# The first loads in another order, and the second mixer's output projection in split matmuls with part of its weight preparation on GpSimd

## The reference

```python
def first_block(x, ...):
    h = rmsnorm(x, mix_pre_g)
    u, v_s, q, k, v_a, g_a, g_b, f_logit = jnp.split(h @ w_in, IN_SPLITS, axis=-1)
    y_a = spatial_gating(gelu(u), gelu(v_s), w_spatial, b_spatial, sgu_norm_g)
    y_b = forgetting_attention(q, k, v_a, f_logit, b_forget)
    x = x + rmsnorm((sigmoid(g_a) * y_a + sigmoid(g_b) * y_b) @ w_out, mix_post_g)
    return x + rmsnorm(swiglu(rmsnorm(x, ffn_pre_g), w_gate, w_up, w_down), ffn_post_g)

def second_block(x, mem, ...):
    hn = rmsnorm(x, norm_mix_g)
    u_pool, m_q, m_k, m_v, m_o, m_i, m_f, a_q, a_k, a_v = jnp.split(hn @ w_in_2, ...)
    y_pool  = pool_mixer(u_pool, pool_w, pool_scale)           # width 256
    y_mlstm = mlstm_mixer(m_q, m_k, m_v, m_o, m_i, m_f, ...)   # width 256
    y_attn  = attn_mixer(a_q, a_k, a_v, ...)                   # 8 query heads of 64, 2 key heads, rotated
    x = x + jnp.concatenate([y_pool, y_mlstm, y_attn], axis=-1) @ w_out_2   # the projection that changes
    x = x + mem_cross_attn(rmsnorm(x), mem, ca_wq, ca_wkv, ca_wo)
    x = x + ec_moe(rmsnorm(x), router_w, w_gu, w_down)         # 16 experts, 32 tokens each
    return rmsnorm(x, final_norm_g)
```

## Time and profile before

| | |
|---|---|
| runs | 1501.70, 1501.83, 1503.94 us (median 1501.83) |
| profiled execution | 1501.2 us, its span 1499.4 us, mean granted clock 0.875 |
| busy share of the span | PE 81%, its weight load 48%, DVE 27%, ACT 20%, GpSimd (POOL) 3% |
| DMA | 500.9 MB, 334 GB/s over the span |
| chain that ended last | PE 49%, DMA 46%, DVE 2%, ACT 1% |

### The profile page before, as it was taken

How to read it: one execution, slowest core, us unless ns; L and a number is a source line. 1 busy time by engine, 2 the same in 40 slices (tenths; PEclk the granted TensorE clock), 3 DMA queues, 4 the chain that set the end, 5 groups by cost and what they waited for, 6 DMA issues and landing times.

```text
span 1499.4 us, 16367 instructions
## 1 busy us (share of the span) xinstructions
PE 1220.6 (81%) x7015; PEld 713.6 (48%) x7015; DVE 404.0 (27%) x601; ACT 307.0 (20%) x433; POOL 37.8 (3%) x41
## 2 busy tenths in 40 slices
PE   8999999999999999986775775776757857757675
PEld 7888888888878566332231331331322313313232
DVE  5756465665367654000000000000000000000001
ACT  5544444444265552000000000000000000000001
POOL 1000000000031100000000000000000000000000
PEclk9999999999999999886787778778878687787799
DMA  9745436555544388999999999999999999999996
GB/s 340 264 169 170 167 113 206 188 176 218 195 142 128 110 324 345 420 428 429 426 427 427 427 428 428 427 429 427 427 427 429 427 429 427 427 427 428 427 427 283
DMA packets 85347, 500.91 MB, mean 334 GB/s; under 512 B 4990, under 2 KB 30020, under 8 KB 60596
## 3 DMA queue, kind: packets, MB, share of 16 engines
q1 hardware_dynamic: 84084, 495.60, 81.9%
q0 software_dynamic: 1216, 4.63, 0.9%
HBM read 499.16 MB, written 1.05 MB: 334 GB/s over the span
## 4 chain that ended last, share of the span: by engine, by line
PE 49%; DMA 46%; DVE 2%; ACT 1%; issue 0%; POOL 0%; SPq 0%; POOLq 0%; DVEq 0%; ACTq 0%
DMA arena<-in_expert_w_gu_dram 34%; DMA arena<-in_expert_w_down_dram 11%; PE psA L655 9%; PE psB L1346 5%; PE psB L1299 4%; PE psB L888 4%; PE psA L694 4%; PE psB L694 3%; PE psB L1256 3%; PE psA L698 2%; PE psA L1071 2%; PE psB L698 2%; PE psA L899 1%; PE psA L666 1%; PE psA L1006 1%; PE psA L1135 1%
## 5 line engine op out<-in xcount | busy, mean ns | idle before, releaser
L1299 PE MATMUL psB<-arena,x_res 128*32 128x512 f32 x2048 | 323.9, 766 | 200.8 <-DMA arena<-in_expert_w_gu_dram 200.8
L1299 PEld LDWEIGHTS psB<-arena,x_res 128*32 128x32 f32 x2048 | 63.1, 125 | 432.7 <-DMA arena<-in_expert_w_gu_dram 311.1
L1853 DVE TENSOR_TENSOR split_r<-arena,split_r 128x2048 fp32r<-128x2048 f32 x75 | 171.7, 2292 | 109.9 <-ACT split_r L1387 109.6
L1737 ACT ACTIVATE x_res<-psB 128x512 f32<-128x512 f32 x16 | 9.6, 597 | 840.6 <-PE psB L1299 840.6
L1387 ACT CAST split_r<-arena 128x2048 fp32r<-128x2048 f32 x76 | 145.0, 1912 | 102.5 <-PE psA L655 52.7
L655 PE MATMUL psA<-split_r,hT_r 128*128 128x512 f32 x664 | 154.2, 391 | 0.0
L1346 PE MATMUL psB<-arena 128*32 128x512 f32 x1008 | 143.0, 723 | 10.2 <-DMA arena<-in_expert_w_down_dram 9.9
L655 PEld LDWEIGHTS psA<-split_r,hT_r 128*128 128x128 f32 x664 | 123.7, 188 | 25.5 <-issue 0.2
L1256 PE MATMUL psB<-sb_b,arena 128*128 (+1 forms) x512 | 104.7, 382 | 11.4 <-ACT arena L1739 11.3
L1256 PEld LDWEIGHTS psB<-sb_b,arena 128*128 128x128 f32 x512 | 102.4, 310 | 17.8 <-issue 14.2
L2381 DVE TENSOR_TENSOR x_res<-x_res,psB 128x512 f32<-128x512 f32 x16 | 16.4, 1026 | 282.7 <-ACT x_res L1737 282.7
(11 more groups left out here) (396 smaller groups left out, 1086.9 us busy)
## 6 DMA issues: line engine op xcount, KB each, us to landing
arena<-in_expert_w_gu_dram SPq DMA_DIRECT2D x128, 2048.0 KB, 35.3
arena<-in_expert_w_down_dram SPq DMA_DIRECT2D x62, 2048.0 KB, 36.2
arena<-in_w_in_dram SPq DMA_DIRECT2D x35, 1024.0 KB, 7.8
arena<-in_w_gate_dram SPq DMA_DIRECT2D x11, 1024.0 KB, 5.5
arena<-in_w_up_dram SPq DMA_DIRECT2D x11, 1024.0 KB, 8.1
arena<-in_w_down_dram SPq DMA_DIRECT2D x10, 1024.0 KB, 6.6
arena<-in_w_out_dram SPq DMA_DIRECT2D x6, 1024.0 KB, 6.2
arena<-in_ca_wkv_dram SPq DMA_DIRECT2D x4, 1024.0 KB, 6.2
```

The costliest lines, as they stand in the source:

```text
L1299: ins = pe.matmul(psB[32 * j:32 * j + 32, o, :], XC[:, k, :], w[4 * o + j], start=(k == 0), stop=(k == GU_SLOTS - 1), skip_group_check=True)
L1853: v.tensor_tensor(W_LO[n % 2].rearrange("p (k n) -> p k n", **shape), view, W_HI[n % 2].bitcast(F32).rearrange("p (k n) -> p k n", **shape ...
```

## The change

It does these things:

- **Start.** `WS` is loaded after `u0` instead of ahead of the constants. GpSimd issues the forget bias, the forget weights and the second block's gate weights first, then the first gain; it waits for these and for `WS` and the constants, and issues the second gain, the broadcast rows, the router and the pool weights after that. DVE's wait before the gate split is for three small transfers (the wait for all six is further on). ACT begins with a Square of one element. PE's first pass takes the high and the low operand of each half before the next half.
- **Projection.** `wout20` and `wout21` (column halves) become `w2a` and `w2b` (row blocks, 1024 wide, four rows each in two pieces). Each row is 12 split matmuls of 512 columns: high and low weights with the high operand `YT`, high weights with the low operand `YL`. DVE makes `YL` (`rest`). The order of the rows is 0, 1, 4, 5, 6, 7, 2, 3.
- **Who splits them.** `w2a/0`: high ACT, low GpSimd. `w2a/1` and `w2b/0`: high and low GpSimd. `w2b/1`: high ACT, low DVE. `wq` is split in two steps, the second after the operand of the cross attention.
- **Order on PE.** The queries are transposed ahead of the band product, the keys behind it. The pool's product goes to another bank. The keys move to another tile (`KK`).
- **Expert loads.** The last dense load (`wo`) is issued after expert load 0; load 3 waits for `w2b`'s low parts, load 4 for `wq`'s.

The core of the diff:

```diff
@@ loads (SP)
+        w = A["w_out_2"][0]
+        for name, k0, i0, at0 in (("w2a", 0, 0, 0), ("w2b", 2, 2, 2)):
+            add(name, ..., halves=D)
+        W2_ROW = {0: ("w2a", 0, 0), 1: ("w2a", 0, 1), 4: ("w2a", 1, 0), 5: ("w2a", 1, 1),
+                  6: ("w2b", 0, 0), 7: ("w2b", 0, 1), 2: ("w2b", 1, 0), 3: ("w2b", 1, 1)}
...
             load(0)
             load(1)
-            sp.dma_start(WS, A["w_spatial_t"]).then_inc(sig("consts_loaded"), 16)
             sp.dma_start(cst[:, P:NCONST], A["consts"][:, P:NCONST]).then_inc(sig("consts_loaded"), 16)
             for i in range(2, N_DENSE - 1):
                 load(i)
                 if i == 2:
+                    sp.dma_start(WS, A["w_spatial_t"]).then_inc(sig("consts_loaded"), 16)
...
             sp.wait_ge(sig("pool_mm"), 2)
             expert_load(0)
+            load(N_DENSE - 1)
             sp.wait_ge(sig("ym_ready"), 1)
             expert_load(2)
             sp.wait_ge(sig("ym_tr"), 1)
             expert_load(1)
+            for n, _ in pieces["w2b"]:
+                sp.wait_ge(*lo_signal(n))
+            expert_load(3)
             sp.wait_ge(*lo_signal(pieces["wq"][-1][0]))
-            expert_load(3)
-            load(N_DENSE - 1)
-            after_slot(sp, "wout21")
             expert_load(4)
@@ PE
-                for k in range(h):
-                    pe.wait_ge(sig("xh_ready"), k // 2 + 1)
-                    pe.wait_ge(*((sig("first_cast"), 1) if k < h // 2 else (sig("hi_ready"), 1)))
-                    for t in range(TT):
-                        pe.matmul(psA[:, 2 * pair + t, :], HTS[0][:, k, t * P:(t + 1) * P], w[:, k, :], ...)
+                for b, quarter in enumerate(("first_cast", "hi_ready")):
+                    pe.wait_ge(sig(quarter), 1)
+                    for i, x_ready in enumerate(("xh_ready", "xl_ready")):
+                        pe.wait_ge(sig(x_ready), b + 1)
+                        for k in (2 * b, 2 * b + 1):
+                            for t in range(TT):
+                                pe.matmul(psA[:, 2 * pair + t, :], HTS[i][:, k, t * P:(t + 1) * P], w[:, k, :], ...)
...
+            pe.wait_ge(sig("aq_ready"), 2)
+            pe.wait_ge(sig("rope_ready"), 2)
+            pe.wait_ge(sig("om_ready"), ML_H)
+            for i in range(4):
+                for t in range(TT):
+                    ins = pe.transpose(psB[:, i // 2, ...], RQ[:, t, i, :], ident)
...
             def at_turn(i):
-                if i >= 1:
-                    pe.wait_ge(sig("yt_ready"), 1 + i)
+                pe.wait_ge(sig("xl_ready"), YL_FIRST + 1 + i)
...
             def merged_rows(k, count):
+                pe.wait_ge(sig("hi_ready"), n + 1)
+                pe.wait_ge(*lo_signal(n))
                 pe.wait_ge(sig("yt_ready"), count)
-                for t in range(TT):
-                    for c in range(2):
-                        merged(k, t, c)
+                    for j, w in enumerate((w_hi, w_lo)):
+                        for t in range(TT):
+                            for c in range(2):
+                                pe.matmul(psA[:, 2 * c + t, :], YT[:, k, ...], w[:, r, ...], ...)
+                    pe.wait_ge(sig("xl_ready"), YL_FIRST + count)
...
+                        ins = pe.matmul(psA[:, 2 * c + t, :], YL[k][:, ...], w_hi[:, r, ...], ...)
@@ ACT
+            act.wait_ge(sig("pair_zeroed"), 1)
+            a.activation(junkA[:, 0:1], c_pair[:, 0:1].bitcast(F32), ACT.Square)
...
             a.activation(OG, OG, ACT.Sigmoid).then_inc(sig("mvo_ready"), 1)
+            split_hi("w2a", 0)
...
+            act.wait_ge(sig("hi_ready"), pieces["w2b"][0][0] + 1)
+            split_hi("w2b", 1)
             at_turned(3)
...
-            split_hi("wq")
-            at_out(3)
+            split_hi("wq", 0)
...
             operand_hi("n4", ROW["norm_mem_g_2"], dst=HT4)
+            split_hi("wq", 1)
@@ GpSimd
-            for name in ("k2", "ml", "n4"):
+            root("k2")
+            def split_hi(name, b):
+                n, view = pieces[name][b]
+                pool.wait_ge(loaded_sem(where[name]), loaded_no(where[name]))
+                pool.wait_ge(sig("hi_ready"), n)
+                pool.wait_ge(sig("piece_used"), n - 1)
+                nc.gpsimd.tensor_copy(W_HI[n % 2]..., view).then_inc(sig("hi_ready"), 1)
+
+            split_lo("w2a", 0)
+            split_hi("w2a", 1)
+            split_lo("w2a", 1)
+            split_hi("w2b", 0)
+            split_lo("w2b", 0)
+            for name in ("ml", "n4"):
                 root(name)
@@ DVE
-            dve.wait_ge(sig("small_loaded"), 16 * 6)
+            dve.wait_ge(sig("small_loaded"), 16 * 3)
...
+            def rest(k, count, src, scale=None):
+                dve.wait_ge(sig("yt_ready"), count)
+                hi = YT[:, k, :].bitcast(F32)
+                if scale is None:
+                    return v.tensor_tensor(YL[k], src, hi, ALU.subtract)
+                return v.scalar_tensor_tensor(YL[k], src, scale, hi, ALU.mult, ALU.subtract)
+
             for i in range(AT_H // 2):
+                if i >= 2:
+                    rest(2 + i, i, psB[:, 2, 0:TOK]).then_inc(sig("xl_ready"), 1)
                 dve.wait_ge(sig("s2_mm"), i + 1)
                 for g in range(AT_KV):
                     row_max("s2", i + 4 * g, g)
+                    if i == 0 and g == 0:
+                        (rest of rows 0 and 1)
...
-            split_lo("wq")
+            split_lo("w2b", 1)
+            (rests of rows 7, 2, 3)
+            split_lo("wq", 0)
```

More of the change, by code:

```diff
@@ L390, in build @@
         N_PLAIN = X_SLOTS + len(plain_no)
[L392 to L393 removed]
+        ring_of = {name: where[name] % SLOTS for name in ("w2b", "wq", "wo")}
+        turning = (7, 5, ring_of["w2b"], ring_of["wq"], 6, ring_of["wo"], 3, 4)
         ONCE = {2: X_SLOTS + 1, 7: X_SLOTS, 10: None}
@@ L462, in turned_last, with rest_no @@
             return (psA[:, 1, 0:TOK], psA[:, 3, 0:TOK], psB[:, 1, 0:TOK], psB[:, 3, 0:TOK])[b]
+        POOL_LO = [pieces[name][b][0] for name, b in (("mqk", 0), ("mqk", 1), ("w2a", 0), ("w2a", 1), ("w2b", 0))]
         def lo_signal(n):
[L466 to L469, removed]
+            if n in POOL_LO:
+                return sig("lo2_ready"), POOL_LO.index(n) + 1
+            return sig("lo_ready"), n + 1 - sum(i < n for i in POOL_LO)
+        YL_FIRST, YL_COUNT = 4 * SPLIT_TURNS.index("n4"), 6
+        def rest_no(tag, b):
+            return SPLIT_TURNS.index(tag) * 4 + b + 1 + YL_COUNT * (tag == "n4")
         def loaded_no(i):
@@ L496, in load @@
                     if last in pieces:
-                        sp.wait_ge(*lo_signal(pieces[last][-1][0]))
+                        for n, _ in pieces[last]:
+                            sp.wait_ge(*lo_signal(n))
                     else:
@@ L1068, in at_values @@
                 ins.then_inc(sig("pv2_mm"), 1)
-            def merged(k, t, c):
-                return pe.matmul(psA[:, 2 * c + t, :], YT[:, k, t * P:(t + 1) * P], ws[c][:, k, :],
-                                 start=(k == 0), stop=(k == KT - 1))
             def merged_rows(k, count):
-                pe.wait_ge(sig("yt_ready"), count)
+                name, b, r = W2_ROW[k]
+                n = pieces[name][b][0]
+                if (b, r) == (0, 0):
+                    assert where[name] == used[0]
+                    used[0] += 1
@@ new lines, in merged_rows @@
+                w_hi, w_lo = (part[n % 2].rearrange("p (k n) -> p k n", n=D) for part in (W_HI, W_LO))
+                pe.wait_ge(sig("hi_ready"), n + 1)
+                pe.wait_ge(*lo_signal(n))
+                pe.wait_ge(sig("yt_ready"), count)
+                last = k == 3
+                if last:
+                    pe.wait_ge(sig("xl_ready"), YL_FIRST + count)
+                else:
+                    for j, w in enumerate((w_hi, w_lo)):
+                        for t in range(TT):
+                            for c in range(2):
+                                pe.matmul(psA[:, 2 * c + t, :], YT[:, k, t * P:(t + 1) * P], w[:, r, c * NC:(c + 1) * NC],
+                                          start=(k == 0 and j == 0), stop=False)
+                    pe.wait_ge(sig("xl_ready"), YL_FIRST + count)
@@ L2246, in _ @@
                     row_max("s2", i + 4 * g, g)
+                    if i == 0 and g == 0:
+                        for k in range(2):
+                            r = ROW["pool_scale_2"] + k
+                            ins = rest(k, 1, psB[:, 3, k * TOK:(k + 1) * TOK], cols[:, r:r + 1])
+                        ins.then_inc(sig("xl_ready"), 1)
                 ml_out(i)
```

115 lines of the change are left out of this document (69 added, 46 removed).

## The result

| | before | after |
|---|---|---|
| median | 1501.76 us (1500.79 to 1503.94, 4 runs) | 1513.69 us (1511.43 to 1514.13, 4 runs) |
| ratio | | 1.0077, 95% interval 1.0064 to 1.0090 |
| span of the profiled execution | 1499.4 us | 1511.4 us |

The changed kernel is slower by 11.9 us; 1513 was forecast.

A forecast was written before the change was run, and what follows sets the result against it. The time was taken as the router's end, set by PE, plus a constant. Terms -2.2 - 3.0 + 10.7 + 1.5 + 4.0 = +11.0 on 1501.2 gave 1512.2, stated as 1513 since that execution lay 0.6 below the median; range 1498 to 1518.

The forecast's parts named there:

- What bounds the kernel: Whole kernel: the time is the router's end plus a constant; a microsecond on PE before 588 moves the end by one.
- The first loads: Start: reordered loads let the gate product start at 31.5 instead of 33.64, -2.2 us (bounds -1 and -3).
- The output projection: Projection rows: split matmuls take 2.74 us a row instead of 3.44; after losses -3.0 us (bounds -1 and -5.6).
- The key chain: Key rotation before scores(0): GpSimd's w2a splits and cast hold DVE's operations, +10.7 us (bounds +3 and +13).
- The clock: First scores and rows behind PE's hole: half clock expected, +1.5 us (bounds 0 and +3).
- The second collision: Turns 1 and 2: GpSimd's cast and low split of w2b/0 hold DVE, +4.0 us (bounds 0 and +6).
- The sum: Whole kernel: the five terms add to +11.0 us, 1512.2 on the profiled execution's 1501.2, stated as 1513.
- Slower by less: Rival, key rotation: GpSimd loses the race in the gaps, only the first split blocks; +1.7, 1502.9 us, chance 0.13.
- Faster: Rival, key rotation: GpSimd and DVE don't exclude one another for these operands; -5.4, 1495.8 us, chance 0.21.
- It doesn't do what it says: Rival, start: gate product still waits, for the spatial weights; 1.0 won, not 2.2; 1513.4; within the main case's 0.66.
- the signs that I had named: Rotation: DVE products over 4 and over 2 us, PE hole about 10 us, clock falling; load 11 issued near 603.

The follow-up runs named there:

- nothing new on GpSimd: The changed kernel with all three new casts on ACT and all three low splits on DVE: 1499.80 us against 1500.54 for the kernel before, ratio 0.9990.
- free low parts: The changed kernel without new GpSimd work, DVE writing one column in place of each of three low splits (output not the reference's): 1494.76 us, ratio 0.9944.
- the first loads alone: The kernel before with only the reordered start (loads, Square, first pass, waits): 1498.64 us, ratio 0.9985; again on another chip 1498.36 us, ratio 0.9972.
- The split behind the keys: The changed kernel with GpSimd's first low split waiting until the keys are rotated: 1505.47 us, ratio to the kernel before 1.0026.
- the half of the rows that fitted: The changed kernel, only rows 6, 7, 2, 3 split, no new GpSimd work, first w2b piece prepared earlier: 1495.59 us, ratio to the kernel before 0.9958.
- one added product: The kernel before plus one GpSimd subtraction of 128x2048 behind the root of the key norm, result unread: 1507.78 us, ratio 1.0040.
- one added cast: The kernel before plus one GpSimd one-input copy of 128x2048 behind the root of the key norm: 1502.67 us, ratio 1.0007.

## Why the prediction was right, point by point

- **What bounds the kernel.** The time is PE's before the router plus a constant: from the issue of load 11 to the end of the span it is 905.6 to 908.2 us in all thirteen profiles (907.1 before, 906.3 after). The spread of 2.6 us is what one profile leaves open.
- **The first loads**, -2.2: -1.5 in the profiled pair. The gate split was done at 31.6, as I had it, but PE was busy with the first pass until 32.16, not 31.1. Its first matmul didn't start sooner: 10.28, and in the run with nothing new on GpSimd, where x landed as in the kernel before, 9.62; DVE's first cast there ran at 8.83, not at 8.20 as in the kernel before, for its weights landed later. The difference 33.64 - 31.5 was itself 2.1, written as 2.2. In the medians the term is -1.9 and -4.4; the part that comes with a late x I couldn't see in one profile.
- **The output projection**, -3.0: from turn 3 to the cross attention 16.7 us for 18.6, -1.9; the three rows within the turns -1.4; turn 0 loses 0.4 to the rests. That is -2.9. With free low parts -2.3 was measured on the same stretch, with waits of 0.57 and 0.49 in the turns that the changed kernel didn't have. A row took 2.8 to 3.0, a little over my 2.74.
- **The key chain**, +10.7: DVE's last key products started at 502.17 for 493.41, 10.2 late net of the start, and the query transposes ahead of the band product gave back 0.4 (from gate product to scores(0) 462.1 us with nothing new on GpSimd, 462.6 with the first loads alone): +9.8. The working was right in kind, whole instructions in turns, and the first product caught (at 490.36) was the seventh of the fifteen operations, the one where I had put the root's end; the cast measured 1.89, not 2.4, and the splits 4.5. The Trainium skill (GPSIMD Engine Reference, section on which engine to use for what) had led to an estimate of 1.7 for the cast, closer to the measured 1.89 than my 2.4.
- **The clock**, +1.5: this term was mis-sized. Half clock cost 0.8 in front of scores(0) (2.5 us from the key transposes to them, 1.8 in the run with nothing new on GpSimd), 0.8 in turn 0, and 2.5 behind the second hole (0.9 in the transposes, 1.65 in row 4): 4.1. I had allowed for it behind one hole only.
- **The second collision**, +4.0: 5.1. The last scaling did wait for the low split, and the one before it for the cast; whether scalings are held I had left open. The split behind the keys shows that the small products ahead of them in DVE's line are caught just as well.
- **What wasn't in the sum**: 2.4 us lie between the 14.5 at the cross attention and the 12.0 at the end. 1.6 of them are the slow first expert matmuls of the one profile of the kernel before, and 0.8 lie behind load 11, within the spread of 2.6 there. Neither is a gain of the change.
- **The sum**, measured: -1.5 - 2.9 + 9.8 + 4.1 + 5.1 - 2.4 = +12.2, against 12.0 between the two spans and +11.0 forecast. The number was right in part by luck: clock and collision were 3.7 too small together, and what offset them was a key chain that I had 0.9 too dear and 2.4 of difference between two executions. The medians are 11.9 apart, like the spans; but against the three other profiles with the old order the profiled execution of the kernel before was 2.7 to 3.1 us early behind the gate product and 1.6 late at the experts, which partly cancel. One pair of profiles doesn't settle these terms to better than some 2 us.
- **The rivals.** "Slower by less" fell: GpSimd won each race in the gaps. "Faster" fell with the first DVE product of 4.50. "It doesn't do what it says" fell: the gate product had no wait. Of the signs that I had named, two products over 4 us and one of 1.91, a hole of 10.2 us and the fall of the clock came; load 11 was issued at 605.1 for 603. (The 1513.4 of that third rival counts from 1512.2; counted like the forecast of 1513 it is 1514.)

## What to carry to other kernels

Before a long cast or subtraction is given to GpSimd, look at what DVE does at that time. Beside such an instruction of 2048 columns every DVE product of two SBUF tiles that met one, down to two columns, and the two fp32 scalings that met one stood until GpSimd's instruction ended, and a row of them let one such DVE instruction through at a time. GpSimd's roots, of 4 columns here, held nothing. A chain of short DVE steps on the critical path (rotation, norms) is the worst neighbour; copies and row maxima that read PSUM are a harmless one (0.42 and 0.69 us, as without it). When an engine is relieved inside a loop of turns, count the idle time of the next one per turn first: here 1.84 us of DVE were the whole room, and the version with the half of the rows that fitted won 1.9 us on PE (506.0 to 504.1, 0.4 of it by the order of the transposes), where all of them lost 2.3.

## What the runs showed that I had not expected

- Behind a hole of 4.3 us (one added product) the ten key and query transposes took 2.39, behind one of 1.7 us (one added cast) 1.31. Up to scores(0) the clock added some 2 us to the 4.3 of the first; behind the 5.1 us of the second collision it added 2.5. So a hole can cost more than its own time.
- x lands at different times (PE's first transposes at 5.2 to 6.3 us). In the old order the three profiles with a late x, by 0.7 to 0.8 us, had a gate product that started 1.3 to 1.9 later and ran 1.2 to 1.5 longer; in the new order its start moved by 1.5 us in all and its length not at all.
- The stretch from cross attention to load 11 had two lengths in thirteen profiles, 51.0 and 52.6 us, and the one profile that a forecast is read from can have either.
